# Gathering routed tokens in fp32 straight into turned form, in a one-core streaming encoder step

## The reference, cut to what matters

```python
logits = (x2d @ w_router + b_router).astype(jnp.float32)
top_val, top_idx = lax.top_k(logits, TOP_K)
gates = jax.nn.softmax(top_val, axis=-1)
...
def expert_block(args):
    xb, e = args                              # the tokens that chose expert e
    gu = xb @ w_gate_up[e] + b_gate_up[e]     # 1024 -> 2048
    gate = jnp.minimum(gu[:, :D_FF], SWIGLU_LIMIT)
    up = jnp.clip(gu[:, D_FF:], -SWIGLU_LIMIT, SWIGLU_LIMIT)
    hid = (up + 1.0) * (gate * jax.nn.sigmoid(SWIGLU_ALPHA * gate))
    return hid @ w_down[e] + b_down[e]        # 1024 -> 1024
...
return jnp.zeros_like(x2d).at[tok].add(w_sorted[:, None] * ys[dest])
```

## Time and profile before

| | |
|---|---|
| median of three runs | 1218.29 us (1217.98 to 1221.67) |
| the profiled execution | 1219.33 us |
| its span, first to last instruction | 1217.5 us |
| TensorE busy | 1125.7 us (92%) |
| VectorE busy | 387.3 us (32%) |
| ScalarE busy | 232.8 us (19%) |
| GpSimd busy | 39.5 us (3%) |
| moved by DMA | 430.73 MB, mean 354 GB/s |

### The profile page before, as it was taken

The page is one execution under the profiler, slowest core; times in us unless marked ns, Lnnn a source line. Parts: engine busy times, 40 slices in busy tenths (PEclk is TensorE's granted clock), DMA queues, the critical chain, the costliest instruction groups (busy, mean ns, idle before and its releaser), DMA issues.

```text
span 1217.5 us, 14744 instructions
## 1 busy us (share of the span) xinstructions
PE 1125.7 (92%) x5871; PEld 462.0 (38%) x5871; DVE 387.3 (32%) x838; ACT 232.8 (19%) x370; POOL 39.5 (3%) x23
## 2 busy tenths in 40 slices
PE   5999989899999999999989898989898989899986
PEld 4775655433333333333323232323232323233333
DVE  5568975621313212121212121212130303031234
ACT  3531114412020101111111111111202020211124
POOL 3340000100000000000000000000000000000000
PEclk9998999699999999999999999999999999999998
DMA  9913121699999999999999999999999999999911
GB/s 288 365 37 139 43 104 42 239 386 430 428 427 428 430 428 428 428 430 427 429 428 429 428 428 428 430 428 429 428 429 428 429 428 430 428 428 428 427 44 39
DMA packets 44057, 430.73 MB, mean 354 GB/s; under 512 B 4885, under 2 KB 8933, under 8 KB 19359
## 3 DMA queue, kind: packets, MB, share of 16 engines
q1 hardware_dynamic: 39016, 425.42, 83.7%
q10 hardware_dynamic: 5015, 4.95, 1.2%
HBM read 428.53 MB, written 1.83 MB: 353 GB/s over the span
## 4 chain that ended last, share of the span: by engine, by line
PE 68%; DMA 26%; DVE 3%; ACT 1%; issue 1%; SPq 0%; ACTq 0%; DVEq 0%
PE ps L779 34%; DMA ring<-in_w_gate_up 24%; PE ps L480 7%; PE ps L470 5%; PE ps L739 5%; PE ps L704 4%; PE ps L798 4%; DMA ring<-in_w_down 2%; PE ps L714 2%; PE ps L788 1%; PE ps L504 1%; PE ps L747 1%; PE ps L544 1%; PE ps L562 1%; PE ps L706 1%
## 5 line engine op out<-in xcount | busy, mean ns | idle before, releaser
L779 PE MATMUL ps<-ring,arena 128*64 128x512 f32 x2048 | 466.7, 598 | 19.4 <-DMA ring<-in_w_gate_up 19.4
L798 PE MATMUL ps<-ring,arena 128*64 128x512 f32 x1024 | 232.3, 598 | 30.8 <-DMA ring<-in_w_down 13.6
L779 PEld LDWEIGHTS ps<-ring,arena 128*64 128x64 f32 x2048 | 136.5, 137 | 296.0 <-issue 255.7
L798 PEld LDWEIGHTS ps<-ring,arena 128*64 128x64 f32 x1024 | 68.5, 137 | 171.2 <-issue 113.6
L1694 DVE TENSOR_TENSOR acc<-ps,acc 128x512 f32<-128x512 f32 x64 | 44.2, 691 | 212.8 <-PE ps L739 212.8
L1580 DVE CAST arena<-cst 96x128 bf16 (+1 forms) x17 | 3.8, 222 | 273.0 <-PE ps L779 273.0
L1104 ACT COPY arena<-ps 128x512 f32<-128x512 f32 x32 | 18.7, 586 | 328.9 <-PE ps L788 328.9
L480 PE MATMUL ps<-ring,arena 128*128 128x512 f32 x140 | 64.3, 615 | 1.1 <-DVE arena L1472 1.1
L470 PE MATMUL ps<-arena,ring 128*128 128x288 f32 x256 | 64.2, 410 | 0.7 <-DVE arena L1249 0.7
L1599 DVE TENSOR_TENSOR arena<-ps,par 128x256 f32<-128x256 f32 x68 | 25.5, 417 | 121.5 <-PE ps L779 118.4
L739 PE MATMUL ps<-arena 128*128 128x512 f32 x128 | 63.5, 619 | 0.0
(11 more groups left out here) (267 smaller groups left out, 799.9 us busy)
## 6 DMA issues: line engine op xcount, KB each, us to landing
ring<-in_w_gate_up SPq DMA_DIRECT2D x128, 2048.0 KB, 24.4
ring<-in_w_down SPq DMA_DIRECT2D x64, 2048.0 KB, 23.1
ring<-in_w_in SPq DMA_DIRECT2D x5, 2048.0 KB, 20.5
ring<-in_w_out SPq DMA_DIRECT2D x2, 2048.0 KB, 15.8
ring<-in_w_in SPq DMA_DIRECT2D x2, 1024.0 KB, 11.9
arena<-in_w_ple_gate ACTq DMA_DIRECT2D x2, 768.0 KB, 5.6
arena<-in_w_ple_gate ACTq DMA_DIRECT2D x1, 1280.0 KB, 10.2
acc<-in_x_prompt SPq DMA_DIRECT2D x2, 512.0 KB, 4.5
```

Source lines behind the costliest of these rows:

```text
L779: t = mm(ps[h * 64:h * 64 + 64, G + 2 * e + g, :], xT[:, 2 * kk + c, e * 64:e * 64 + 64], w[:, c, lo:lo + 512], start=False, stop=(kk == 3 ...
L798: t = mm(ps[n * 64:n * 64 + 64, PP + e, :], hidT[:, 4 * e + c, half * 64:half * 64 + 64], w[:, c, n * 512:(n + 1) * 512], start=(half == 0 ...
```

## The change

The tokens stay as they are, fp32, in `xn2`, which moves to the space of the pieces. The one-hot matrix `sel` is fp32. For each of the eight column groups the gather now takes 128 token columns (every second one of 256) as the stationary operand and the one-hot matrix as the moving one, so that the result comes out turned. It goes from PSUM straight to `tokens_out`. The casts, remainders, `copy_gathered` and `turn_tokens` are gone, and so are GpSimd's two operations and the two copies of block 2's positions. The semaphore `gath_mm` is raised after column groups 3 and 7; `tokens_out` waits on it.

```diff
-        xs_s = sb("xs_s", D // 2)
+        sam = sb("sam", D // 2)
...
+        sel = blocks(sam[:, 0:NB * P])
...
-        xn2 = blocks(arena[:, A_CONV + 2 * D:A_CONV + 5 * D])
+        xn2 = blocks(xs[:, 0:NB * D])
...
             def gather(j):
                 pe.wait_ge(S["sel_ready"], j + 1)
-                for n in range(2):
-                    cols = slice(n * 512, (n + 1) * 512)
-                    for b in range(2):
-                        for k in range(3):
-                            mm(ps[:, PP + n, :], selb[:, b, :], xsb[:, b, k, cols],
-                               start=(b == 0 and k == 0), stop=False)
-                    mm(ps[:, PP + n, :], selb[0:96, 2, :], xssb[0:96, cols],
-                       start=False, stop=True).then_inc(S["gath_mm"], 1)
-
-            def turn_tokens(j):
-                for n in range(2):
-                    pe.wait_ge(S["gath_ev"], j * 2 + (n + 1))
-                    for c in range(4 * n, 4 * n + 4):
-                        lo = 256 * (c // 2) + c % 2
-                        t = tr(ps[:, PP + n, (c % 4) * P:(c % 4 + 1) * P], gath[:, lo:lo + 255:2], ident)
-                    t.then_inc(S["xt3_mm"], 1)
-
-            pe.wait_ge(S["xs_l"], NB)
+                for c in range(DC):
+                    lo = 256 * (c // 2) + c % 2
+                    for b in range(NB):
+                        t = mm(ps[:, PP + c // 4, (c % 4) * P:(c % 4 + 1) * P],
+                               xn2[0:ROWS[b], b, lo:lo + 255:2], sel[0:ROWS[b], b, :],
+                               start=(b == 0), stop=(b == NB - 1), skip_group_check=True)
+                    if c % 4 == 3:
+                        t.then_inc(S["gath_mm"], 1)
+
+            pe.wait_ge(S["xn2_ready"], NB)
             gather(0)
-            turn_tokens(0)
...
                 gate_up(3)
-                turn_tokens(j + 1)
                 gate_up(4)
...
-            high(0)
-            middle(0)
             tokens_hi(0)
             square_of(1)
-            low(0)
...
-            high(1)
-            high(2)
-            middle(1)
-            middle(2)
-            act.wait_ge(S["xs_m"], NB)
-            copy(xssb[DEC:2 * DEC, :], mtmp)
-            low(1)
-            low(2)
...
-                copy_gathered(j + 1)
...
-            G.tensor_tensor(rest, rest, xssb[0:DEC, :], ALU.subtract).then_inc(S["xs_rh_s"], 1)
-            G.tensor_tensor(rest, rest, mtmp, ALU.subtract).then_inc(S["xs_rm_s"], 1)
...
-            remainder(0, 0)
-            remainder(0, 1)
-            remainder(1, 0)
-            remainder(1, 1)
...
-            V.tensor_copy(posm[DEC:2 * DEC, 2, 0:E], posm[0:DEC, 2, 0:E])
-            link(V.tensor_copy(posm[2 * DEC:3 * DEC, 2, 0:E], posm[0:DEC, 2, 0:E]))
...
-                V.tensor_tensor(selb.rearrange("p b (e s) -> p (b e) s", e=2), iota_s, per_slot(cur),
+                V.tensor_tensor(sel.rearrange("p b (e s) -> p (b e) s", e=2), iota_s, per_slot(cur),
                                 ALU.is_equal).then_inc(S["sel_ready"], 1)
...
-                    dve.wait_ge(S["xt3_mm"], j * 2 + (n + 1))
+                    dve.wait_ge(S["gath_mm"], j * 2 + (n + 1))
```

More of the change, by code:

```diff
@@ L214, in program @@
         csq = blocks(U_flat[:, 0:H * T], H)
-        Ss = xs_s[:, 0:W]
+        Ss = sam[:, 0:W]
+        sel = blocks(sam[:, 0:NB * P])
         ubs = KdT_flat[:, 0:H * T]
@@ L227, in program @@
         croot = xs[:, 2016:2016 + T]
-        xn2 = blocks(arena[:, A_CONV + 2 * D:A_CONV + 5 * D])
-        junk2 = arena[:, A_CONV + 5 * D:A_CONV + 6 * D]
+        xn2 = blocks(xs[:, 0:NB * D])
+        junk2 = arena[:, A_CONV:A_CONV + D]
         wr = arena[:, A_QD:A_QD + DC * E]
@@ L232, in program @@
         bres = arena[0:96, A_ST:A_ST + D]
-        mtmp = arena[0:DEC, A_CONV:A_CONV + D // 2].bitcast(BF16)
         def h4(x):
@@ L244, in ex @@
             return arena[:, at2[0] - n:at2[0]]
-        gath = ex(D)
         xT = blocks(ex(D), DC)
+        selg = blocks(ex(NB * P))
+        oneh = ex(P // 2).bitcast(BF16)
+        ex(64)
+        gw = ex(T)
+        ex(D - 64 - T - NB * P - P // 2)
         gbuf, sgm, ubuf = ex(D), ex(D), ex(D)
@@ L251, in program @@
         ybuf = ex(D)
[L252 to L255, removed]
         eye = cst[:, C_EYE:C_EYE + E + 2]
@@ L261, in program @@
         junk3, nfin = xs[:, 0:D], xs[:, D:2 * D]
-        xsb = xs[:, :].bitcast(BF16).rearrange("p (b k n) -> p b k n", b=2, k=3)
-        xssb = xs_s[:, :].bitcast(BF16)
         biasb = bias[:, :].bitcast(BF16)
@@ L292, in program @@
             "out_mm", "x2_ready", "pl_mm", "xn2_ready", "xt2_mm", "lg_mm", "top_ready",
-            "wexp", "msk_ready", "gat_ready", "pos_mm", "table_ready", "xs_h", "xs_rh", "xs_rh_s", "xs_m",
-            "xs_rm", "xs_rm_s", "xs_l", "gT_mm", "wr_ready", "x2_lo", "x2_hi", "bias_ready", "zero_ready",
+            "wexp", "msk_ready", "gat_ready", "pos_mm", "table_ready", "gT_mm", "wr_ready", "x2_lo", "x2_hi", "bias_ready", "zero_ready",
             "gw_zero",
             "unit_done", "oneh_ready", "sel_cur", "sel_ready", "selg_cur", "selg_ready",
-            "gath_mm", "gath_ev",
-            "xt3_mm", "xt_ev", "gate_ready", "sig_ready", "up_ready", "gs_ready", "hid_ready", "hidt_mm",
+            "gath_mm", "xt_ev", "gate_ready", "sig_ready", "up_ready", "gs_ready", "hid_ready", "hidt_mm",
             "hidt_ev", "y_ev", "gw_mm", "gw_ev", "comb_mm", "comb_add",
@@ L1021, in _ @@
             act.dma_start(ybuf[0:E, :], a["b_down"][0]).then_inc(S["bd_in"], 16)
[L1024 to L1043, removed]
             def tokens_hi(b):
@@ L1080, in _ @@
                    accum_out=wsum[:, b:b + 1]).then_inc(S["wexp"], 1)
[L1082 to L1085, removed]
             per_layer(4)
@@ L1091, in _ @@
             gate_chunks(gate0, 0, FREE, 0)
-            copy_gathered(0)
             act.wait_ge(S["gT_mm"], 1)
@@ L1188, in _ @@
                 nc.gpsimd.tensor_tensor(lk, kf, lev, ALU.mult).then_inc(S["lev_k"], 1)
-            G = nc.gpsimd
-            rest = xn2[0:DEC, 2, :]
-            pool.wait_ge(S["xs_h"], NB)
-            G.tensor_tensor(rest, rest, xssb[0:DEC, :], ALU.subtract).then_inc(S["xs_rh_s"], 1)
-            pool.wait_ge(S["xs_rh_s"], 1)
-            pool.wait_ge(S["xs_m"], NB)
-            G.tensor_tensor(rest, rest, mtmp, ALU.subtract).then_inc(S["xs_rm_s"], 1)
         @block.vector
@@ L1499, in tokens_lo @@
                               ).then_inc(S["x2_lo"], 1)
[L1501 to L1505, removed]
             residual(0)
```

## The result

The change makes the kernel slower. The median is 1247.99 us (1244.19 to 1254.38, four runs) beside 1219.98 us of the kernel before in the same series: a ratio of 1.023, 95% interval 1.017 to 1.029, so it is clear of the noise. The forecast was 1219.7 us with a range of 1214 to 1225. What came is nearest to rival 4, TensorE as the bound. The profiled execution has a span of 1249.6 us, 32.1 more than before; it is one of the longer of the four, and the medians lie 28.0 apart.

A forecast was written before the change was run, and what follows sets the result against it. The prediction took the weights' DMA to bound the loop, 58.74 us a pair, with TensorE 3.7 us faster. Its terms, -1.1 + 2.2 + 0.3 = +1.4 us on the median of 1218.29, gave 1219.7 us, range 1214 to 1225.

The forecast's parts named there:

- rival 4: In the loop, TensorE becomes the bound if a gather exceeds 7.3 us; at 0.203 per record 42 us more, 1261; chance 0.08.
- The count of the gather's records: In each new gather: 24 fp32 products of two records each, 48 records.
- Their spacing: Between the new gather's records on TensorE: 0.12 us at full clock, 5.8 us a gather; ends 5.2 and 9.7 us.
- Gather(0) and the clock: Before the loop: gather(0) starts at half clock, which rises 5.3 us in; 8.4 us, loop starts 1.1 us earlier.
- rival 2: Clock high at gather(0), 5.8 us: 1217.1 (chance 0.12), or 1214.6 with the flow in time (chance 0.11).
- GpSimd and the position copies: Between router and loop: removing GpSimd's operation gains 1.93 us on VectorE's L1540, removing two position copies 0.4 us.
- The flow of weights: First pair of the loop: slots freed later, so continuous weight transfer begins 2.2 us later after the loop's start.
- unit 11: Loop's end: TensorE, now waiting 1.13 us for this unit's weights, has 1.5 us more work and comes 0.3 late.
- The sum: Whole kernel: -1.1 at the loop's start, +2.2 for the flow, +0.3 at the last unit, +1.4 us in all.

The follow-up runs named there:

- pad_rows: Changed kernel with block 2's gather product taking all 128 rows, zeros above 32, so every product has the same rows; 1214.12 us, ratio 0.9953 to the kernel before.
- gpsimd_back: The kernel with equal rows (pad_rows) with two GpSimd operations of 32 x 1024 put back while VectorE chooses the experts; 1219.25 us.
- extra4: pad_rows with four more fp32 products of 128 x 128 x 128 before every gather but the first; 1220.05 us, ratio 0.9987 to the kernel before.
- extra16: pad_rows with sixteen more fp32 products of 128 x 128 x 128 before every gather but the first; 1253.15 us.
- plain_columns: Changed kernel with 128 adjacent token columns as the gather's weights instead of every second one; 1244.52 us.

## Why the prediction was wrong

**The count of the gather's records** was right: 48.

**Their spacing** is the step that failed: "The new gather has no wait inside, so I take 0.12: 48 x 0.12 = 5.8 us at the full clock." Measured 8.75 us. 0.12 is what a record costs when all have the same rows (pad_rows 5.85 us). The rows that I took as near, L544 and L714, are runs of records with equal rows. The new gather is 128, 128, 32 rows, eight times over. The one row of that form, L822 with 128, 128 and 32, stood among mine at 0.203, and I used it as a far upper end instead of asking what made it dear. Reckoned as the others were, with the tail of its last record (0.25) taken off, it is (0.61 - 0.25) / 2 = 0.18, just what came. So rival 4 got 0.08 where it was the case, though its threshold of 0.15 a record was about right (the measured 0.182 lies beyond it) and its price of 42 us at 0.203 is in proportion to the loop's 26.

The rule from the Trainium skill ("TensorE: Matmul & The Clock Gate", Part 3), that a weight load passes under a running product only when the row groups differ, fits these runs the other way round. Among equal rows it is hidden (0.118 a record, streaming alone 0.108), and at each change between 128 rows and 32 or 64 it stands bare (0.2 us).

**Gather(0) and the clock.** The prediction had 8.4 us and a rise of the clock within it; rival 2 saw that the clock could be high at the start. Both happened partly: it was high at the start, fell during the gather and stayed low. 13.35 us. With equal rows rival 2's full case came true: 5.9 us. But rival 2's reason, the shorter pause before the position products, isn't what raised the clock: it was up at 222.6, ahead of that pause. That it was up at the gather is luck for rival 2.

**GpSimd and the position copies.** Expected: 1.93 and 0.4 us. The comparison takes 0.56 us after the change, and the way to gather(0) is 3.16 us shorter, 0.8 more than the sum, since the position products ran at the full clock. Right in size. gpsimd_back shows GpSimd's operations delaying VectorE by as much (2.1 us), though there they held two other operations and not the comparison.

**The flow of weights.** "The flow becomes continuous 2.2 us later after the loop's start", and unit 11 0.3 late: 2.5 us. With the gather at the predicted size (pad_rows) the loop was 0.9 us longer than before. The sign was right, the size was not. The bound by weights held at 57.3 us a pair (extra4) and was gone at 59.97 (extra16); where between them it ends, no run shows.

**The sum.** Had the spacing been 0.12 the answer would still have been 4 or 5 us too high: -4.5 at the loop's start (-1.1 predicted), +0.9 in the loop (+2.5 predicted), and 1214 to 1216 measured.

## What to carry to other kernels

Price a run of small products by its sequence and not by one product: write down the rows of each weight load in order, and look in the trace for a run with the same pattern. A block with fewer rows between full ones may be cheaper when padded with zeros, or when all such blocks are put together. An engine that has 3.7 us of slack in a period of 58.7 is a bound in waiting: where a change adds work to it, its price needs an upper end that is checked against that slack.

## What the runs showed of the hardware

- A change of rows between 128 and 32, or 128 and 64, makes one weight load 0.2 us late; the starts of the products show it as 0.1 us on each of two records. At half clock the records around it are 0.35 to 0.38 us apart, the others 0.21.
- The granted clock fell in a run of small products with bare weight loads, 2.3 us after TensorE's last pause (229.4 in the changed kernel), and stayed at half for 17 us with TensorE recorded as busy for nearly all of it. The same products with covered loads kept 2.4 GHz in seven profiles of eight.
- GpSimd's `tensor_tensor` of 32 x 1024 held VectorE's `tensor_scalar` of 128 x 3 and a cast of 128 x 24 elements, 1.01 and 1.45 us instead of 0.17 and 0.18.
- Weights read with a step of two fp32 columns cost 0.006 us more a record than adjacent ones (0.118 beside 0.112 us in plain_columns, and 0.111 in the added products of extra16).
